# Layer 0's input in a second, column-major copy: the split of x at the start of a two-layer decoder step

## What is computed

```python
for l in range(2):
    h = rmsnorm(x, norm_mix[l])                    # x * rsqrt(mean(x*x)) * gain
    z = h @ w_in[l]                                # 1024 -> 2560: u | q | k | v | g
    pool_out = pool_mix(u, ...)                    # trailing means, then a small matmul per group
    ret_out = silu(g) * groupnorm(retention(q, k, v, state))
    x = x + concat(pool_out, ret_out) @ w_out[l]
    x = x + hier_moe(rmsnorm(x, norm_ffn[l]))      # 16 experts, 2 per token
y = rmsnorm(x, norm_final)
```

## Time and profile before

| What | Value |
|---|---|
| Median of 3 runs | 862.34 us (861.26 to 864.4) |
| Span of the profiled execution (first to last instruction) | 859.6 us |
| PE busy | 834.1 us, 97% of the span |
| DVE busy | 603.5 us, 70% |
| ACT busy | 479.2 us, 56% |
| POOL busy | 309.4 us, 36% |
| Mean DMA rate | 217 GB/s |
| TensorE clock granted, mean | 0.992 of full |

### The profile page before, as it was taken

How to read it: one execution, slowest core, us unless ns; L and a number is a source line. 1 busy time by engine, 2 the same in 40 slices (tenths; PEclk the granted TensorE clock), 3 DMA queues, 4 the chain that set the end, 5 groups by cost and what they waited for, 6 DMA issues and landing times.

```text
span 859.6 us, 12214 instructions
## 1 busy us (share of the span) xinstructions
PE 834.1 (97%) x4221; PEld 667.4 (78%) x4221; DVE 603.5 (70%) x953; ACT 479.2 (56%) x817; POOL 309.4 (36%) x199
## 2 busy tenths in 40 slices
PE   8999999999988999999899999999999999999995
PEld 5887888888857888888478887889887678888862
DVE  3435546555687999998664455556647899999957
ACT  3633442612456888887544333352335588888863
POOL 0014993301032577532000199803101227745110
PEclk9999999999999999999999999999999999999998
DMA  8522223323938999995864222322288599999839
GB/s 295 168 74 82 74 73 86 100 62 124 415 120 321 384 343 389 389 374 200 286 171 152 71 79 67 94 63 65 87 299 327 165 415 333 364 390 382 329 111 342
DMA packets 73182, 186.27 MB, mean 217 GB/s; under 512 B 15884, under 2 KB 30732, under 8 KB 64794
## 3 DMA queue, kind: packets, MB, share of 16 engines
q1 hardware_dynamic: 59034, 153.26, 50.5%
q0 software_dynamic: 10368, 23.09, 7.5%
q10 hardware_dynamic: 3728, 9.26, 2.8%
HBM read 170.56 MB, written 29.91 MB: 233 GB/s over the span
## 4 chain that ended last, share of the span: by engine, by line
PE 84%; DVE 8%; DMA 4%; ACT 2%; issue 1%; POOLq 0%; ACTq 0%; DVEq 0%
PE ps L421 14%; PE ps L425 11%; PE ps L424 11%; PE ps L1280 10%; PE ps L1282 9%; PE ps L1281 9%; PE ps L1287 3%; PE ps L423 3%; PE ps L1258 2%; PE ps L1481 2%; DVE x L1973 1%; DMA hg<-xn_d,rowidx 1%; DMA back<-y_d 1%; PE ps L1446 1%; PE ps L1421 1%
## 5 line engine op out<-in xcount | busy, mean ns | idle before, releaser
L421 PE MATMUL ps<-wh,hT 128*128 128x512 f32 x480 | 193.7, 404 | 3.3 <-DVE lT L1808 2.7
L782 POOL DMA_INDIRECT y_d<-y,rowidx x32 | 113.6, 3550 | 116.6 <-DVE y L1894 114.3
L1874 DVE TENSOR_TENSOR gul<-wgu,eh 128x1024 fp32r<-128x1024 f32 x128 | 150.4, 1215 | 4.1 <-ACT eh L991 4.1
L425 PE MATMUL ps<-wh,lT 128*128 128x512 f32 x384 | 150.1, 391 | 0.0
L424 PE MATMUL ps<-wl,hT 128*128 128x512 f32 x384 | 149.9, 390 | 0.0
L991 ACT ACTIVATE eh<-wgu 128x1024 fp32r<-128x1024 f32 x128 | 128.8, 1057 | 10.2 <-PE ps L1282 8.8
L1865 DVE SCALAR_TENSOR_TENSOR wl<-raw,gcol,wh 128x512 fp32r<-128x512 f32 x80 | 75.7, 951 | 80.5 <-ACT wh L964 80.4
L421 PEld LDWEIGHTS ps<-wh,hT 128*128 128x128 f32 x480 | 90.3, 188 | 23.9 <-DVE lT L1808 5.2
L1280 PE MATMUL ps<-eh,hgTh 128*128 128x512 f32 x240 | 96.3, 401 | 0.4 <-issue 0.4
L964 ACT ACTIVATE wh<-raw,gcol 128x512 fp32r<-128x512 f32 x80 | 57.4, 721 | 65.3 <-PE ps L423 50.1
L1282 PE MATMUL ps<-eh,hgTl 128*128 128x512 f32 x240 | 93.7, 391 | 0.0
(11 more groups left out here) (231 smaller groups left out, 1553.6 us busy)
## 6 DMA issues: line engine op xcount, KB each, us to landing
wgu<-in_gate_up SPq DMA_DIRECT2D x64, 1024.0 KB, 12.4
wdn<-in_w_down SPq DMA_DIRECT2D x64, 512.0 KB, 11.9
raw<-in_w_in SPq DMA_DIRECT2D x80, 256.0 KB, 2.7
raw<-in_w_out SPq DMA_DIRECT2D x32, 256.0 KB, 3.0
back<-y_d SPq DMA_DIRECT2D x14, 512.0 KB, 7.5
xn_d<-xf ACTq DMA_DIRECT2D x10, 512.0 KB, 4.8
s<-in_state_ret POOLq DMA_DIRECT2D x8, 512.0 KB, 5.2
x<-in_x_prompt SPq DMA_DIRECT2D x4, 512.0 KB, 6.2
```

Of the source, the lines that this page charges most:

```text
L421: pe.matmul(out, both, w_h, start=first, stop=False)
L425: return pe.matmul(out, l[:, t * P:(t + 1) * P], w_h, start=False, stop=final)
L782: pool.indirect_dma_start(out=y_d, out_offset=bass.IndirectOffsetOnAxis(ap=rowidx[:, 1, e:e + 1], axis=0), in_=y[s][:, :], in_offset=None, ...
L1874: ve.tensor_tensor(gu_pair(gul, gul3, e, s, p), gu_pair(wgu, wgu3, e, s, p), gu_split(e, p)[:, :].bitcast(F32), ALU.subtract).then_inc(glo, 1)
```

## The change

The host passes x once more, with columns as rows: `x_cols`, eight blocks of 128 columns by 576 tokens. For layer 0 each block is loaded into a new tile `x_in` (in space that is free at that time), and `hT` and `lT` are made from it, one block per step, without PE: ACT rounds it (`first_hi`), DVE subtracts (`first_lo`, in two parts, the 64 sample tokens and the 512 prompt tokens). Block 0's high part is made by DVE. PE drops layer 0's forty transposes and does all five tiles per step from step 0 on; in step 0 its matmuls are in an order of their own (`first_block`). `EARLY[0]` is 0. The row-major x is loaded later, in iterations 5 to 9 of SP, its squares are taken in iterations 7 to 9 of ACT and the root in iteration 10, just ahead of the first evacuations. The constants, now with `ident` in one load, are issued in iteration 8, the small tables in iteration 9. The idle turns go from ten to nine. Layer 1 keeps its way; only the counts that its waits compare with are shifted. The core of the diff, first the constants and the tile, then the lists of SP, ACT, PE and DVE in this order:

```diff
-EARLY = (RAW, RAW + 1)
+EARLY = (0, RAW + 1)
+SQUARE_AT = ({7: (LAST, 0), 8: (1, 2), 9: (3,)}, {RAW + t: (t,) for t in range(NT)})
+ROOT_AT = (10, RAW + NT)
+        x_in = tile("x_in", [P, KC, SEQ + NSAMP], off=shared)
```

```diff
-            load_x(0)
-            for s in range(RAW):
-                load_raw(0, s)
-            for t in range(1, NT):
-                load_x(t)
-            sp.dma_start(cst[:, P:], a["cst"][:, P:]).then_inc(cst_ld, 16)
-            sp.dma_start(tri[:, :], a["tri"]).then_inc(cst_ld, 16)
+            def load_xt(k):
+                if k >= LAST:
+                    sp.wait_ge(lo_done, k - LAST + 2)
+                sp.dma_start(x_in[:, k, :], a["x_cols"][k]).then_inc(row_ld[k % LAST], 16)
+
+            def first_loads(s):
+                if s == 3:
+                    load_xt(4)
+                    load_xt(5)
+                if s == 4:
+                    load_xt(6)
+                    load_xt(7)
+                if s == 5:
+                    load_x(LAST)
+                if s >= 6 and s < 10:
+                    sp.wait_ge(lo_done, s - 6 + LAST + 2)
+                    load_x(s - 6)
+                if s == 8:
+                    sp.dma_start(cst[:, :], a["cst"]).then_inc(cst_ld, 16)
+                    sp.dma_start(tri[:, :], a["tri"]).then_inc(cst_ld, 16)
+
+            load_raw(0, 0)
+            load_xt(1)
+            load_raw(0, 1)
+            load_xt(2)
+            load_raw(0, 2)
+            load_xt(3)
             for L in range(NL):
                 for s in range(RAW, WIN_STEPS):
                     if s >= EARLY[L]:
                         load_raw(L, s)
-                    if s == 6:
+                    if L == 0:
+                        first_loads(s)
+                    if s == (6 if L else 9):
```

```diff
-            sc.dma_start(cst[:, 0:P], a["cst"][:, 0:P]).then_inc(table_ld, 16)
-            sc.dma_start(gcol[:, :, :, :], a["gcol"]).then_inc(table_ld, 16)
+            def first_hi(k):
+                sc.wait_ge(row_ld[k % LAST], 16 * (k // LAST + 1))
+                sc.activation(hT[:, k, 0:SEQ + NSAMP], x_in[:, k, :], ACT.Copy).then_inc(hi_done, 1)
+
+            sc.dma_start(gcol[:, :, :, :], a["gcol"]).then_inc(gcol_ld, 16)
+            sc.dma_start(x_in[:, 0, :], a["x_cols"][0]).then_inc(row_ld[0], 16)
...
+                    sc.wait_ge(gcol_ld, 16)
                     w_hi(0, 0)
+                    sc.wait_ge(hi_done, 1)
+                    for s in range(1, RAW):
+                        first_hi(s)
+                        w_hi(0, s)
...
+                    if L == 0 and s < KC:
+                        first_hi(s)
                     if s >= EARLY[L]:
                         w_hi(L, s)
-                    if s - RAW < NT:
-                        mix_square(L, s - RAW)
-                    if s - RAW == NT:
+                    for t in SQUARE_AT[L].get(s, ()):
+                        mix_square(L, t)
+                    if s == ROOT_AT[L]:
                         mix_root(L)
```

```diff
+            def first_block(s):
+                pe.wait_ge(hi_done, s + 1)
+                if s:
+                    pe.wait_ge(lo_done, s + 2)
+                    for t in range(NT):
+                        win_mm(0, s, t)
+                    return
+                pe.wait_ge(whi, 1)
+                for t in range(LAST):
+                    pe.matmul(ps[t][:, :], hT[:, 0, t * P:(t + 1) * P], wh[0][:, :], start=True, stop=False)
+                pe.wait_ge(lo_done, 1)
+                both = hT[:, 0, SEQ:TOK]
+                pe.matmul(ps[LAST][:, :], both, wh[0][:, :], start=True, stop=False)
+                pe.wait_ge(wlo, 1)
+                for t in range(NT):
+                    pe.matmul(ps[t][:, :], hT[:, 0, t * P:(t + 1) * P], wl[0][:, :], start=False, stop=False)
+                pe.wait_ge(lo_done, 2)
+                for t in range(LAST):
+                    last = pe.matmul(ps[t][:, :], lT[:, 0, t * P:(t + 1) * P], wh[0][:, :], start=False, stop=False)
+                last.then_inc(wpe, 1)
...
-            idle_turns(4, 10)
+            idle_turns(7, 9)
```

```diff
+            def first_lo(k):
+                if k:
+                    ve.wait_ge(hi_done, k + 1)
+                last = ve.tensor_tensor(hT[:, k, LO_LAST], x_in[:, k, HI_LAST], hT[:, k, HI_LAST].bitcast(F32), ALU.subtract)
+                if k == 0:
+                    last.then_inc(lo_done, 1)
+                    w_lo(0, 0)
+                ve.tensor_tensor(lT[:, k, 0:SEQ], x_in[:, k, 0:SEQ], hT[:, k, 0:SEQ].bitcast(F32), ALU.subtract).then_inc(lo_done, 1)
...
+                    ve.wait_ge(gcol_ld, 16)
+                    ve.wait_ge(row_ld[0], 16)
+                    ve.tensor_copy(hT[:, 0, 0:SEQ + NSAMP], x_in[:, 0, :]).then_inc(hi_done, 1)
+                    ve.wait_ge(hi_done, 1)
+                    first_lo(0)
+                    for s in range(1, RAW):
+                        first_lo(s)
+                        w_lo(0, s)
                 for s in range(RAW, WIN_STEPS + 4):
+                    if L == 0 and s < KC:
+                        first_lo(s)
                     if s >= EARLY[L]:
                         w_lo(L, s)
+                    if L == 0 and s == KC:
+                        ve.wait_ge(cst_ld, 32)
-                    if s == RAW + NT + 1:
+                    if s == (10 if L == 0 else RAW + NT + 1):
                         mix_scale(L)
```

More of the change, by code:

```diff
@@ L308, in sem @@
             return ctx.enter_context(nc.semaphore(name))
-        cst_ld = sem("cst_ld"); row_ld = [sem(f"row_ld{t}") for t in range(NT)]; gain_ld = sem("gain_ld"); table_ld = sem("table_ld")
+        cst_ld = sem("cst_ld"); row_ld = [sem(f"row_ld{t}") for t in range(NT)]; gain_ld = sem("gain_ld"); gcol_ld = sem("gcol_ld")
         small_ld = sem("small_ld"); raw_ld = [sem(f"raw_ld{i}") for i in range(RAW)]
@@ L400, in end_loads, with row_loads, mix_hi_done, mix_lo_done @@
             return 64 * (L + 1) + (48 if L + 1 == NL else 0)
+        def row_loads(t):
+            return 32 if t < LAST else 0
+        def mix_hi_done(L):
+            return 15 * L - 2
+        def mix_lo_done(L):
+            return 15 * L - 1
+        def ffn_hi_done(L):
+            return 15 * L + KC
+        def ffn_lo_done(L):
+            return 15 * L + KC + 1
         def squares(i):
@@ L1261, in mix_rows @@
             def mix_rows(L, t, halves=range(2)):
-                pe.wait_ge(table_ld, 32)
-                if t or not L:
+                if t:
                     x_there(pe, L, t)
@@ L1508, in _ @@
             pe.wait_ge(still_set, 1)
-            idle_turns(4, 10)
+            idle_turns(7, 9)
             for L in range(NL):
-                mix_rows(L, 0, (0,) if L else range(2))
                 if L:
+                    mix_rows(L, 0, (0,))
                     idle_turns(0, 6)
[L1515 to L1521, removed]
-                            mix_rows(L, t + 1)
-                pe.wait_ge(lo_done, 15 * L + 2 * NT)
-                for s in range(EARLY[L], WIN_STEPS):
-                    for t in range(NT):
-                        win_mm(L, s, t)
+                    for t in range(NT):
+                        pe.wait_ge(lo_done, mix_lo_done(L) + 2 * t + 1)
+                        for s in range(EARLY[L]):
+                            win_mm(L, s, t)
+                            if s == 1 and t == 0:
+                                mix_rows(L, 0, (1,))
+                            if s == (2 if t == 0 else 1) and t + 1 < NT:
+                                mix_rows(L, t + 1)
+                    pe.wait_ge(lo_done, mix_lo_done(L) + 2 * NT)
+                for s in range(EARLY[L], WIN_STEPS):
+                    if L == 0 and s < KC:
+                        first_block(s)
+                    else:
+                        for t in range(NT):
+                            win_mm(L, s, t)
                     if s in U_AT:
```

52 lines of the change are left out of this document (19 added, 33 removed).

## The result

The changed kernel takes 867.2 us (median of 6 runs, 866.18 to 868.8), the kernel before 862.0 (6 runs on the same chip): a ratio of 1.0057, 95% interval 1.0042 to 1.0071. The prediction was 856.6, faster, with a range up to 859.5. The change makes the kernel slower by 5.2 us; the rival called "Slower", which had a chance of 0.04, had named 867. In the fifth experiment two of twelve runs were in a slow state (1397 and 2945 us) and are left out of its ratio (without them its median is 858.9), and its rows are those of a further run, because the profiled one was the first of these two, at a granted clock of 0.55.

The account below looks back on a forecast made before the run. PE was taken to bound the kernel, busy 834.1 of 859.6 us. 7.0 us won at the start, less 0.5 for the evacuation and 0.8 for the clock, gave 862.3 - 5.7 = 856.6 us, range 854.0 to 859.5.

Parts of the forecast that it names:

- Slower: Block 10, root and first evacuation late behind constants, tile 3 and tables; a 12 us stall, 867 us; chance 0.04.
- What goes, and when PE starts: Start of layer 0: 7.9 us of transposes and waits leave PE; its first real matmul comes at 6.55 us.
- DVE and ACT kept pace: Steps after the start: PE's 3.2 us per step hide DVE's and ACT's work; 0.1 us lost, bounds 0 and 0.3.
- The clock at the start: First matmuls: TensorE's clock may rise later after PE's idling; 0.8 us lost, bounds 0 and 1.7.
- The first evacuation: Step 8, tile 1: PE needs a bank at 32.95 us and may wait; 0.5 us lost, bounds 0 and 1.5.
- the sum 7.0 - 0.5 - 0.8: Whole kernel: 7.0 us won by step 3, less 0.5 evacuation wait and 0.8 slow clock, makes 5.7 us.
- the term of 0.5: PE's expected wait in us at step 8, tile 1, for the bank of tile 0; bounds 0 and 1.5.
- The two signs by which the prediction was to be wrong: PE waiting in steps 1 to 7, or the clock staying low over two stretches.
- The start or the roots cost more: Early loads 2 us late, or constants delay tile 3 and block 10 by 2 to 3; 858.6 us, chance 0.15.
- From 23 us on PE does the same as before: Rest of the kernel after the start: PE's work unchanged, so the 5.7 us won would remain.

Follow-up runs that it names:

- the fifth experiment: Changed kernel with small tables behind weight block 10, constants behind block 11, gain row behind block 12: 859.42 us, ratio 0.9969 to the kernel before.
- the first experiment: Changed kernel with the nine small tables issued behind weight block 10 instead of ahead of it: 859.93 us, ratio 0.9977 to the kernel before.
- the first two experiments: Changed kernel with the small tables behind weight block 10, 859.93 us; changed kernel with 30 idle turns in PE's wait at step 8, 863.37 us.

## Why the prediction was wrong, step by step

**What goes, and when PE starts: right.** All 7.9 us left PE. The load took 4.1 for 4.5, the copy 0.46 for 0.75 (it lies between the row that was taken and the lower bound, 0.38). PE's first real matmul came at 5.94 for 6.55. DVE and ACT kept pace: PE does not wait between 5.94 and 34.07 us. The 0.38 us estimated from the Trainium skill's two results per cycle for such a copy ("VectorE: DVE Perf Modes", section "Mode 2×_2P — use both read ports for one tensor") is nearer to the 0.46 us than the row from PSUM was.

**The clock at the start: one bound or the other, not the value taken.** In after the nine slow matmuls cost 9 × 0.2 = 1.8 us, beside 1.7 for the upper bound and 0.8 taken. In nine of the eleven profiles with the new start it cost next to nothing: the same start gave four matmuls in 1.2 us and step 3 at 15.65 in the first experiment, 15.46 with the evacuation ahead. So the start is worth 5.9 us or 7.6 to 7.8, from one profile to the next; the two profiles with the late rise were after and the one with list order and later loads (step 3 at 17.35). That agrees with the sentence of the Trainium skill that the prediction cited ("TensorE: Matmul & The Clock Gate", section "What's actually happening"): the number of slow matmuls varies from run to run. In after it cost little, since PE ran into a wait whose end it hardly sets: with the fast start and the same loads (the idle turns in the wait) that end came 0.6 us sooner, at 40.61.

**The first evacuation: the step that failed.** The prediction named the chain (tables, block 10, root, evacuation), its slack, and that the queue would be full. It then took 31.0 - 23.53 = 7.5 us for the issue of the tables from a stretch with a DMA share of 0.68, and put the full queue only on the landing, as 0 to 1.5 us. The issue itself is what grew: 14.4 us. Block 10 was issued at 35.36, not at 26.7 to 27.7, and from there landed in 3.3 us, nearly the 2.8 assumed. So in the sum 7.0 - 0.5 - 0.8 the term of 0.5 was mis-sized: the wait was 7.1 us. That is shown from three sides: moving the tables behind block 10 ends the wait 5.7 us sooner; one large load put ahead of the same tables in the kernel before stretches them to 12.2 us and makes it slower; and taking the evacuation out of block 10's way gives 858.4 with the slow issue still there. Why SP needs longer for the same instruction is not shown; what goes with it is in the last section. The two signs by which the prediction was to be wrong (a wait in steps 1 to 7, a low clock over two stretches) did not cover a long wait at step 8.

**Tile 3: a step left out of the sum.** The root needs the squares of all tiles, and tile 3's load was costed only as an issue; only a rival, "The start or the roots cost more", had it late, by 2 to 3 us. It was issued at 20.58 behind 1.75 MB of constants (8.4 us from issue to landing) and took 11.2 us. In after this is hidden behind block 10. It is the 3.05 us that stay with the evacuation ahead and some 2.2 of the 3.13 in the first experiment, both with PE there 1.7 to 1.9 us sooner than in after. The constants' share in it is shown by the square's coming at 28.00 and not at 31.80 when they go later.

**The clock after a stall: not priced.** The prediction priced stalls by their length. From the end of the wait to the landmark it takes 6.2 us in before at a full clock, 9.2 in after; after waits of 3.0 to 4.6 us in five other profiles 7.7 to 9.0; after 1.4 and 1.8 us, or with idle turns in the wait, 6.3. So each wait of 3 to 7 us brought a further 1.5 to 3 us here, without a rule by length (2.8 behind a wait of 3.4, 1.7 behind one of 4.6), and those below 2 us brought 0.1.

**Sum.** To the landmark: 5.9 - 7.1 - 2.9 = 4.1 us lost (4.2 measured), where the prediction had 7.0 - 0.5 - 0.8 = 5.7 won. "From 23 us on PE does the same as before" held from the landmark to 411 us within 0.25 us, and not from there on. At the boundary of the layers, where PE waits often, it takes 14.3 to 14.9 us from the idle turns at 411 us to layer 1's first matmul in before, the first two experiments and before with the extra load, where the clock stays at 1.00 from 418 to 440 us, and 15.8 to 17.6 in after and all others, where it is 0.84 to 0.93. What decides it was not tested. It is one reason why kernels that lead by 5 to 6 us at the landmark are only 3 to 5 us ahead by their ratios: near 411 us that lead is still there, 4.0 to 7.2 us, and at layer 1's first matmul it is 1.4 to 4.6.

**The rivals.** "Slower" was the one that happened, and its mechanism was block 10 behind the constants, tile 3 and the tables, as named. That its 867 us agree with the 867.2 measured is luck: it asked for a stall of 12 us, no clock and a start worth 7.0; there were 7.1 us, the clock's 2.9, 1.7 us behind 411 us and a start worth 5.9. Its chance was too low because it was tied to a landing ten microseconds after the issue at 210 GB/s. Block 10 did land late, at 38.6, but 3.3 us after its issue, and the engines moved 359 GB/s from 17.36 to 33 us: it was SP's issue that was late.

With the list order mended, the change wins, but less than forecast: 858.4 us against 856.6, ratio 0.9957, which is 3.7 us where 5.7 were forecast (the interval, 0.9937 to 0.9977, goes from 2.0 to 5.4).

## What to carry to other kernels

The time that a queue needs to issue small loads is not a constant of theirs: read it in a stretch as full as the one they are moved to, or bound it by the slowest one seen, and put small tables behind the loads that something waits for. On another queue they are off the sequencer's list, but their transfers can still delay the loads beside them, as block 7 shows. In a list that an engine does in order, work that frees a buffer for the bounding engine goes ahead of work that waits for a transfer. And a stall of TensorE that lasts some microseconds is priced with the slow matmuls behind it, here 1.5 to 2.9 us for waits of 3.0 to 7.1. The length of a wait also depends on when the engine came to it, so two kernels are compared by when the wait ends.

## What the runs showed of the hardware that was not expected

- SP needed 7.5 us to issue the nine tables in before. With the constants ahead of them it needed 13.5 to 14.9 in five profiles (after, and the experiments with the tables behind block 10, with turns in the wait, with twelve turns and with the list order alone), and 12.2 in before with the extra load. With the constants behind them it needed 8.0 to 11.4 in four. So 3.0 to 6.4 of the 6.9 us of growth in after go with the constants, though the tables' place in the list differs between these runs too; what makes the rest was not tested, and neither was why an issue takes longer.
- The growth is not spread evenly, and not always on the same table. The expert router's (64 KB) took 1.36 us in before, 4.26 to 4.57 in the five profiles and 3.80 in before with the extra load, but also 2.48 to 4.93 with the constants behind it. `gnrow` took 0.51 in before, 2.69 to 3.00 in four of the five and 3.62 with the extra load, and 0.50 to 1.01 with the constants behind it; in the fifth (twelve turns) it took 0.54, and the group router's table, 0.4 to 1.4 elsewhere, took 2.77. From POOL's queue the expert router's took 0.94.
- With the same instructions up to there, TensorE's clock rose at different times. Nine idle turns took 4.02 us in after and 3.42 to 3.81 in six other profiles, where the last of them already ran faster. In two more the turns took 3.99 and 4.02 us and the first real matmuls were fast all the same. In after and in the run with list order and later loads they were slow until some 10 us.
